# Mixing stage: queries and keys turned by DMA and joined by VectorE

## The reference, cut to what matters

```python
def hybrid_mixer(u, positions, w_in, b_gate, w_branch_moba, w_branch_sb, w_out):
    proj = u @ w_in                                   # 256 x 5120
    q_a, k_a, v_a, q_b, k_b, v_b, g_a, g_b = jnp.split(proj, cuts, axis=-1)
    q_a = partial_rotary(split_heads(q_a, N_HEADS_MOBA), positions)
    k_a = partial_rotary(split_heads(k_a, N_HEADS_MOBA), positions)
    y_a = merge_heads(moba_attention(q_a, k_a, split_heads(v_a, N_HEADS_MOBA)))
    y_b = merge_heads(stick_breaking_attention(split_heads(q_b, N_HEADS_SB),
                                               split_heads(k_b, N_HEADS_SB),
                                               split_heads(v_b, N_HEADS_SB)))
    gates = jax.nn.sigmoid(jnp.concatenate([g_a, g_b], axis=-1) + b_gate)
    merged = gate_a * (y_a @ w_branch_moba) + gate_b * (y_b @ w_branch_sb)
    return merged @ w_out
```

## Time and profile before

| | |
|---|---|
| median of 3 runs | 1204.53 us (1204.47 to 1204.54) |
| the profiled execution | 1204.95 us, its span 1203.0 us |
| TensorE busy | 1195.1 us, granted clock 1.00 in every slice |
| VectorE busy | 780.0 us |
| ScalarE busy | 699.0 us |
| mixing stage in the profile | about 186 to 345 us |

### The profile page before, as it was taken

The page is one execution under the profiler, slowest core; times in us unless marked ns, Lnnn a source line. Parts: engine busy times, 40 slices in busy tenths (PEclk is TensorE's granted clock), DMA queues, the critical chain, the costliest instruction groups (busy, mean ns, idle before and its releaser), DMA issues.

```text
span 1203.0 us, 16864 instructions
## 1 busy us (share of the span) xinstructions
PE 1195.1 (99%) x5622; PEld 986.0 (82%) x5622; DVE 780.0 (65%) x1107; ACT 699.0 (58%) x1030; POOL 73.8 (6%) x119
## 2 busy tenths in 40 slices
PE   9999999999999999999999999999999999999998
PEld 7888888877788888888888788888888887888887
DVE  6656556688686656557778766756556667665554
ACT  7545555566555545558675576645555546755552
POOL 0430000000000000000220110000000000000000
PEclk9999999999999999999999999999999999999999
DMA  9987764554556987755754528977655454876662
GB/s 314 268 235 228 224 200 153 162 168 139 164 193 190 275 248 231 220 179 174 200 171 162 175 60 230 262 226 210 205 175 175 144 163 132 245 225 200 202 200 76
DMA packets 218917, 234.68 MB, mean 195 GB/s; under 512 B 66608, under 2 KB 158896, under 8 KB 218864
## 3 DMA queue, kind: packets, MB, share of 16 engines
q1 hardware_dynamic: 163792, 214.61, 56.9%
q10 hardware_dynamic: 53280, 13.64, 6.3%
q0 software_dynamic: 1792, 5.75, 1.7%
HBM read 219.78 MB, written 1.05 MB: 184 GB/s over the span
## 4 chain that ended last, share of the span: by engine, by line
PE 96%; DMA 2%; DVE 1%; ACT 1%; issue 0%; ACTq 0%; DVEq 0%
PE bank L2035 30%; PE bank L2037 30%; PE bank L2036 30%; PE bank L2094 2%; DMA sb_probs<-sb_probs 1%; PE bank L2248 1%; PE bank L2264 1%; PE bank L2235 1%; PE bank L2233 0%; DMA sb_gates<-h_xT 0%; ACT sb_probs L1277 0%; PE bank L2552 0%; DVE sb_rmax L1930 0%; PE bank L2541 0%; PE bank L2266 0%
## 5 line engine op out<-in xcount | busy, mean ns | idle before, releaser
L1360 DVE TENSOR_TENSOR sb_wl<-sb_raw,sb_wh 128x1024 fp32r<-128x1024 f32 x313 | 376.3, 1222 | 116.5 <-ACT sb_wh L741 111.6
L2035 PE MATMUL bank<-sb_wh,sb_aTh 128*128 128x512 f32 (+1 forms) x1124 | 435.5, 387 | 0.6 <-DVE sb_scores L1423 0.5
L2037 PE MATMUL bank<-sb_wh,sb_aTl 128*128 128x512 f32 (+1 forms) x1124 | 431.0, 383 | 0.0
L2036 PE MATMUL bank<-sb_wl,sb_aTh 128*128 128x512 f32 (+1 forms) x1124 | 430.7, 383 | 0.0
L741 ACT ACTIVATE sb_wh<-sb_raw 128x1024 fp32r<-128x1024 f32 (+1 forms) x319 | 326.9, 1047 | 142.2 <-PE bank L2037 103.0
L2035 PEld LDWEIGHTS bank<-sb_wh,sb_aTh 128*128 128x128 f32 x1124 | 211.3, 188 | 42.2 <-issue 1.4
L2037 PEld LDWEIGHTS bank<-sb_wh,sb_aTl 128*128 128x128 f32 x1124 | 211.2, 188 | 41.9
L2036 PEld LDWEIGHTS bank<-sb_wl,sb_aTh 128*128 128x128 f32 x1124 | 211.4, 188 | 40.1
L1360 DVE TENSOR_TENSOR sb_wl<-sb_z,sb_wh 128x1024 fp32r<-128x1024 f32 x88 | 107.5, 1226 | 56.0 <-ACT sb_wh L741 56.0
L845 ACT ACTIVATE sb_junk<-bank,sb_rstd 128x256 f32<-128x256 f32 x88 | 36.8, 470 | 156.6 <-PE bank L2037 156.3
L1423 DVE SCALAR_TENSOR_TENSOR sb_scores<-bank,sb_rstd,sb_junk 128x256 f32<-128x256 f32 x88 | 38.5, 479 | 115.6 <-ACT sb_junk L845 115.4
(11 more groups left out here) (220 smaller groups left out, 929.1 us busy)
## 6 DMA issues: line engine op xcount, KB each, us to landing
sb_raw<-ffn_w_down SPq DMA_DIRECT2D x80, 256.0 KB, 4.4
sb_raw<-w_in SPq DMA_DIRECT2D x80, 256.0 KB, 3.2
sb_raw<-w_down SPq DMA_DIRECT2D x80, 256.0 KB, 3.9
sb_raw<-w_gate SPq DMA_DIRECT2D x48, 256.0 KB, 3.2
sb_raw<-w_up SPq DMA_DIRECT2D x48, 256.0 KB, 4.0
sb_raw<-ffn_w_gate SPq DMA_DIRECT2D x44, 256.0 KB, 3.6
sb_raw<-ffn_w_up SPq DMA_DIRECT2D x44, 256.0 KB, 4.4
sb_raw<-e_w_in SPq DMA_DIRECT2D x40, 256.0 KB, 3.3
```

Of the source, the lines that this page charges most:

```text
L1360: dve.tensor_tensor(wl[:, u % NSPLIT, :], raws[SLOT[u]], wh[:, u % NSPLIT, :].bitcast(F32), ALU.subtract).then_inc(low_done, 1)
L2035: pe.matmul(dst, lh, w_hi, start=start, stop=False)
L2036: pe.matmul(dst, lh, w_lo, start=False, stop=False)
L2037: return pe.matmul(dst, ll, w_hi, start=False, stop=stop)
```

## The change

TensorE no longer transposes the query and key tiles of the mixing stage. Instead, for each of the four tiles, ScalarE copies the 16-bit halves into a buffer (`qk_split`, two copies of 128x1024, at steps 4, 8, 17, 21) and issues one transposing DMA (`qk_turn`, at steps 5, 9, 19, 23), and VectorE joins the halves into `qkT` (`qk_join`, two copies of 128x1024, at steps 11, 12, 25, 27). TensorE waits for the first two joins ahead of unit 13 and for all four ahead of unit 29, where it had waited for evacuations ahead of units 13 and 25. The tiles used as buffers (`vm0`, `junk`, `qkT[:, 2]`, `qkT[:, 3]`) are free at these times; the fourth turn waits for the third, whose source it overwrites. The factor 0.125 moves from the copies into the addition of the mask: for mixing heads, one instruction multiplies the scores by 0.125 and adds the mask. The core of the diff (new semaphores and the removed code of `qt` and `qt_evac` are left out):

```diff
+        def as_halves(tile):
+            return tile.rearrange("p a c -> p (a c)").bitcast(U16)
+
+        QK_TILES = [0, 1, 3, 4]
+        qk_planes = [as_halves(a) for a in (vm0[:, :, :], qkT[:, 2, :, :], vm0[:, :, :])] + [junk[:, :].bitcast(U16)]
+        qk_planesT = [junk[:, :].bitcast(U16)] + [as_halves(a) for a in (qkT[:, 3, :, :], qkT[:, 3, :, :], vm0[:, :, :])]
...
+            def qk_split(k):
+
+                if k < 2:
+                    act.wait_ge(mix_evac_a, QK_TILES[k] + 1)
+                    act.wait_ge(mix_evac_d, QK_TILES[k] + 1)
+                else:
+                    act.wait_ge(rope_done, k - 1)
+                halves = z[:, :, QK_TILES[k], :].bitcast(U16).rearrange("p t (c h) -> p h t c", h=2)
+                for h in range(2):
+                    ins = copy(qk_planes[k].rearrange("p (h t c) -> p h t c", h=2, t=NT)[:, h], halves[:, h])
+                ins.then_inc(mix_planed, 1)
+
+            def qk_turn(k):
+
+                act.wait_ge(mix_planed, k + 1)
+                if k == 3:
+
+                    act.wait_ge(mix_turned[0], 32)
+                act.dma_start_transpose(qk_planesT[k].rearrange("p (b r) -> p b r", r=P), qk_planes[k]).then_inc(mix_turned[k % 2], 16)
 
...
             for v in range(4, 44):
-                if v == 6:
-                    qt_evac(mix_at, 0, 0.125)
-                if v == 10:
-                    qt_evac(mix_at, 1, 1.0)
+                split(u0 + v)
+                if v in (4, 8):
+                    qk_split(v // 4 - 1)
+                if v in (5, 9):
+                    qk_turn(v // 4 - 1)
+                if v in (17, 21):
+                    qk_split(v // 4 - 2)
+                if v == 19:
+                    qk_turn(2)
                 if v == 23:
-                    qt_evac(mix_at, 2, 0.125)
-                split(u0 + v)
-                if v == 23:
-                    qt_evac(mix_at, 3, 1.0)
+                    qk_turn(3)
                 mix_steps(v)
...
+            def qk_join(k):
+
+                dve.wait_ge(mix_turned[k % 2], 16 + 16 * (k // 2))
+                turned = qk_planesT[k].rearrange("p (h t k r) -> p h k t r", h=2, t=NT, k=4)
+                halves = as_halves(qkT[:, k, :, :]).rearrange("p (k t r h) -> p h k t r", k=4, t=NT, h=2)
+                for h in range(2):
+                    ins = dve.tensor_copy(halves[:, h], turned[:, h])
+                ins.then_inc(mix_joined, 1)
 
...
-                ins = dve.tensor_tensor(s, bank[4 + i % 2][:, 0:384], bias[:, :], ALU.add)
+                if kind == "fox":
+                    ins = dve.tensor_tensor(s, bank[4 + i % 2][:, 0:384], bias[:, :], ALU.add)
+                else:
+                    ins = dve.scalar_tensor_tensor(s, bank[4 + i % 2][:, 0:384], 0.125, bias[:, :], ALU.mult, ALU.add)
...
             for v in range(4, 44):
-                if v == 24:
-                    qt_evac(mix_at, 3, 1.0)
                 if v % 4 == 0 and v <= 24:
                     evac(u0 + v, W_IN_BANKS[v // 4 - 1], 1, z[:, :, v // 4 - 1, :], mix_evac_d)
                 if v in (16, 20):
                     rotate(v // 4 - 1)
-                if v == 6:
-                    qt_evac(mix_at, 0, 0.125)
-                if v == 10:
-                    qt_evac(mix_at, 1, 1.0)
-                if v == 23:
-                    qt_evac(mix_at, 2, 0.125)
                 if v < 13:
                     split(u0 + v)
                 elif v > 13:
                     split(u0 + v - 1)
+                if v in (11, 12):
+                    qk_join(v - 11)
                 mix_steps(v)
+                if v in (25, 27):
+                    qk_join((v - 21) // 2)
...
             for v in range(4, 44):
-                if v == 6:
-                    qt(mix_at, 0, 0, lambda: evacuated(1))
-                if v == 10:
-                    qt(mix_at, 1, 1, lambda: evacuated(2))
                 if v == 13:
 
                     evacuated(3)
-                    pe.wait_ge(mix_at.qt_evac_a, 2)
-                    pe.wait_ge(mix_at.qt_evac_d, 2)
-                if v == 23:
-
-                    pe.wait_ge(mix_at.s_read, 6)
-                    qt(mix_at, 2, 3, lambda: pe.wait_ge(rope_done, 1))
-                if v == 24:
-                    qt(mix_at, 3, 4, lambda: pe.wait_ge(rope_done, 2))
-                if v == 25:
-
-                    pe.wait_ge(mix_at.qt_evac_a, 4)
-                    pe.wait_ge(mix_at.qt_evac_d, 4)
+                    pe.wait_ge(mix_joined, 2)
+                if v == 29:
+
+                    pe.wait_ge(mix_joined, 4)
```

More of the change, by code:

```diff
@@ L341, in two_block_kernel @@
         dve_chain = sem("dve_chain")
+        mix_planed = sem("mix_planed")
+        mix_turned = [sem(f"mix_turned{i}") for i in range(2)]
+        mix_joined = sem("mix_joined")
         mix_evac_a = sem("mix_evac_a")
@@ L397, in __init__ @@
             def __init__(self, tag, stick=False, cross=False):
-                self.qt_psum = sem(tag + "_qt_psum")
-                self.qt_evac_a = sem(tag + "_qt_evac_a")
-                if not cross:
-                    self.qt_evac_d = sem(tag + "_qt_evac_d")
+                if not stick:
+                    self.qt_psum = sem(tag + "_qt_psum")
+                    self.qt_evac_a = sem(tag + "_qt_evac_a")
+                    if not cross:
+                        self.qt_evac_d = sem(tag + "_qt_evac_d")
                 self.s_psum = sem(tag + "_s_psum")
@@ L423, in two_block_kernel @@
         A_LAG = 3
-        QT_BANKS = [6, 6, 4, 4]
         MIX_SCORES = [13, 17, 21, 25, 29, 32, 35, 38]
@@ L987, in _ @@
             rstd_known(1)
-            def qt_evac(at, k, scale):
-                act.wait_ge(at.qt_psum, 2 * k + 1)
-                copy(qkT[:, k, 0:2, :], bank[QT_BANKS[k]][:, :], scale).then_inc(at.qt_evac_a, 1)
+            def qk_split(k):
[13 more added lines that the diff above has]
+                act.dma_start_transpose(qk_planesT[k].rearrange("p (b r) -> p b r", r=P), qk_planes[k]).then_inc(mix_turned[k % 2], 16)
             def mix_high(m):
@@ L1537, in evac @@
                 dve.tensor_scalar(dst[:, 1, :], bank[bank_ + 1][:, :], rs(stat, 1), None, ALU.mult).then_inc(done, 1)
-            def qt_evac(at, k, scale):
-                dve.wait_ge(at.qt_psum, 2 * k + 2)
-                dve.tensor_scalar(qkT[:, k, 2:4, :], bank[QT_BANKS[k] + 1][:, :].rearrange("p (h t) -> p h t", h=2), scale, None, ALU.mult)\
-                   .then_inc(at.qt_evac_d, 1)
+            def qk_join(k):
[5 more added lines that the diff above has]
+                ins.then_inc(mix_joined, 1)
             def rotate(m):
@@ L2200, in _ @@
             u0 = FIRST["w_in"]
-            def qt(at, k, m, ready):
-                ready()
-                if k >= 1:
-                    pe.wait_ge(at.qt_evac_a, k)
-                    pe.wait_ge(at.qt_evac_d, k)
-                for g in range(2):
-                    transposes(bank[QT_BANKS[k] + g], lambda j, t: z[:, t, m, tok(2 * g + j)]).then_inc(at.qt_psum, 1)
             def evacuated(n):
```

## The result

| | before | changed |
|---|---|---|
| median | 1204.53 us (1204.19 to 1205.08, 6 runs) | 1209.04 us (1206.17 to 1210.56, 6 runs) |
| profiled execution | 1204.95 us, span 1203.0 us | 1206.17 us, span 1204.4 us |

The ratio is 1.0034, 95% interval 1.0025 to 1.0044: slower by 4.5 us. The profiled execution, 1206.17 us, is the shortest of the six; the others go up to 1210.56 us, while the kernel before stays within 0.9 us. So the profile after shows the change at its best, and the spread needs an explanation of its own. I first read what the profile shows.

What follows compares the result with a forecast made beforehand. TensorE, busy 1195.1 of 1203.0 us, was taken to bound the kernel. The terms -3.5 + 3.2 + 1.3 = +1.0 us, added to 1204.53 us, gave 1205.5 us, range 1203.8 to 1208.0 us.

Steps and rivals of the forecast that it cites:

- Part 1: Mixing stage: removing TensorE's 32 transposes of four tiles saves 0.88 us a tile, -3.5 us before any new wait.
- Parts 2 and 3: Dropped evacuations of turned tiles on VectorE and ScalarE, and the factor moved into the mask's addition: 0 us each.
- Part 5: Step 13: TensorE waits ahead of unit 13 for tile 1's join, queued behind unit 16's low half on VectorE: +3.2 us.
- Part 6: Step 29: TensorE waits ahead of unit 29 for VectorE's joins 2 and 3: +1.3 us.
- Part 4: ScalarE's splits and turning DMAs fit into its idle time, landing within 8.2 us: 0 us.
- Rival (a): The hole at step 13 lowers TensorE's clock to 1.2 GHz: +1.9 us or a little more, 1207.4 us; chance 0.17.
- (d): Transfers come late: a turn lands over 11 us after start or delays a weight unit: +2 us, 1207.5 us; chance 0.09.

Runs made afterwards that it cites:

- moba_by_dma: Changed kernel, but only tiles 2 and 3 turned by DMA, 0 and 1 by TensorE as before, joins' wait behind unit 29's products: 1203.63 us, ratio 0.9994.
- no_turns_behind: waits_behind without the first two turning DMAs; joins of tiles 0 and 1 read unturned halves, so the output differs: 1202.64 us, ratio 0.9985.
- all_behind: waits_behind with TensorE's wait for tile 2's evacuation also behind unit 13's products and ScalarE's table load behind unit 16's high half: 1201.92 us, ratio 0.9988.
- before_hole: Kernel before the change, plus two join-shaped VectorE copies at step 12 that TensorE awaits ahead of unit 13; no added turns: 1209.62 us, ratio 1.0043.
- fill13: Changed kernel with 14 needless TensorE products directly ahead of its wait for joins 0 and 1, before unit 13: 1207.0 us, ratio 1.0022.
- join1_first: Changed kernel with tile 1's join moved ahead of unit 16's low half in VectorE's queue at step 12: 1209.62 us, ratio 1.0036.
- waits_behind: Changed kernel with TensorE's two waits for joins moved behind the products of units 13 and 29: 1202.92 us (1201.73 to 1207.99), ratio 0.9997.
- sb_by_dma: Changed kernel, but only tiles 0 and 1 turned by DMA, 2 and 3 by TensorE as before, joins' wait behind unit 13's products: 1205.53 us, ratio 1.0015.
- two_more_turns: moba_by_dma plus two needless 0.5 MB turning DMAs issued by ScalarE at steps 31 and 34: 1202.46 us, ratio 0.9986.
- turn0_later: all_behind with tile 0's turning DMA issued at ScalarE's step 7 instead of 5: 1205.51 us (1201.20 to 1207.54), ratio 1.0005.
- after_again: The changed kernel measured once more, nothing altered: 1208.55 us (1207.12 to 1212.19), ratio 1.0035; the profiled execution took 1210.55 us.

## Why the prediction was wrong, point by point

**Part 1 (-3.5 us): right.** moba_by_dma gains 1.80 us in the stage for two tiles, where two times 0.88 was said. The mark that I gave for it, TensorE busy 3.5 us less, was poor: it is 2.3 us less, 3.0 us in the stage, since the last product ahead of a hole and the first behind it count longer than their distance of 0.23 us, and 0.7 us more in the rest of the kernel, which the change doesn't touch. The stage of no_turns_behind, with all four tiles off TensorE, is 3.3 us shorter.

**Parts 2 and 3 (0 us): nothing speaks against them.** The stage of all_behind, -2.9 us with a hole of 0.7 us, leaves no room for another price. They weren't tested by themselves.

**Part 5 (+3.2 us): right in place and size** for the execution profiled first, 3.5 us, and for the hole made in the kernel before, 3.3 us. In before_hole it is also right in its chain: VectorE idles 2.3 us for ScalarE's high half ahead of the low half. In the changed kernel another chain ended last, VectorE's own work since 220.65 us with join 0 in it, which the sum had left out; that it came out only 0.14 us behind the one foretold is luck. And 3.5 us is the smallest of the holes in the profiles of the changed kernel and its near kin, not the only one.

**Part 6 (+1.3 us): right,** 1.1 us, ended by join 3.

So the sum of the parts, +1.0 us, is what the profile shows, +1.3 us in the stage and 1206.17 us in all; and the median is 1209.04 us. The prediction was a sum over an execution in which nothing goes late.

**Part 4 (0 us) is the step that failed,** and with it the clock, which the sum put at nothing and left to a rival (next paragraph). I gave the turning DMAs "room" because ScalarE had idled 3.43 us, and took 8.2 us as the longest landing. The rows with 1.33 and 3.6 us of held queue were there, and I took them for a spread without a cause. In fact the first turn holds the queue for 3.8 to 5.4 us in every profile that has it at step 5, it lands after 8.8 to 13.1 us in the profiles of the changed kernel, the repeat, fill13 and join1_first, and beside it a weight load that took 4.8 us takes 11.0 to 11.6 us in the long executions. ScalarE waited for these loads before, in three waits up to 209 us; I concluded that TensorE would not feel more, because those units are used from 211 us on. In the long executions ScalarE's wait moves to 211 to 215 us and reaches the hole of part 5, which grows from 3.3 to 5.3 and 6.5 us. With the first two turns four of the twelve executions of waits_behind and two of the eleven of sb_by_dma are long (over 1206 us, at a lowered clock); of the kernels that issue no turn at steps 5 and 9 (no_turns_behind, moba_by_dma, two_more_turns) none of thirty-three is. The mark that I had set for this, ScalarE waiting for DMAs after 209 us, is met there and not in the first profile.

**Rival (a) was priced right and given too small a chance.** I said 1.9 us for a fallen clock; eight products at half pace cost 1.7 us. (The products at the kernel's start, from which the price was read, run at half pace while the granted clock of that stretch is given as 1.00; the pace is what the price rests on.) Against it stood that the clock is 1.00 past the short holes; but holes of up to 1.3 us say nothing on one of 3.2 us. In before_hole the mean clock fell in four of five executions.

**Rivals (a) and (d) are not alternatives.** A late transfer makes the hole longer, and the longer hole lowers the clock more surely: in the 1210.55 us execution 3.2 us more hole and 1.7 us of clock, together 4.9 us, where the stage is 4.8 us longer than in the first profile. I gave each a time with the other left out, and so no case came to the 1209 us measured. How the 4.5 us of the median divide can't be read from one profile. From before_hole, 5.1 us for a hole that costs 3.3 us, the clock's share is about 1.8 us; with the +1.3 us of the sum that leaves about 1.4 us for late transfers. This division is worked out, not measured. By it the clock alone would have given 1207.6 us, still inside the range that I stated; the late transfers of part 4 take the median out of it.

**What stays open.** Why the same program has its first turn land after 8.8 us in one execution and 12.5 us in another; the DMA engines are full there (share 0.98 to 1.09), and small shifts may decide who is first, but no run shows it. Whether the held queue or the traffic does more of the harm: turns issued from another engine's queue would part them, and no run has that. And what the long executions of waits_behind, all_behind and turn0_later look like.

## What to carry to other kernels

Put a wait in front of the first instruction that reads the data, not in front of the work ahead of it: moving two waits, each behind one unit's products, was worth some 6 us here, more than the 3.5 us that the change was about. A transposing DMA isn't only its two copies and a landing time: count what it holds in the issuing engine's queue and what loads it meets, and look for several rows of it before taking one. And when each of two hazards would lengthen the same hole, price them together.

## What the runs showed of the hardware

A hole of 3.3 us in TensorE's work lowered the mean granted clock in four of five executions, and at half pace the first eight products cost 1.7 us; in the profiles, holes of up to 2.2 us from start to start (turn0_later) left it at 1.00, those of 3.5 and 3.7 us (before_hole and the changed kernel, the shortest execution of each) did too, and those of 4.5 us (fill13) and 6.9 us (after_again) lowered it to 0.50 and 0.51.

A transposing DMA of 0.5 MB from ScalarE's queue holds it either for 1.3 to 1.4 us or for 1.8 to 4.6 us (5.4 at most), and the count of transposing DMAs before it goes with which. Over all 14 profiles the fast ones of this size are the 15th, 23rd and 27th of an execution, whatever stage they fall in; the 12th to 14th, 24th to 26th, 28th and 30th are slow. Every fourth would fit this, but only the step from two to four more was tested by a run made for it. Those of 0.25 MB take 1.25 us at nearly every place, 2.3 us at most. By the Trainium skill (Advanced Engine Details and Errata, "X-Bar Transpose (TRN2)") transposing DMAs are as fast as regular ones; here, in the changed kernel's profile, a weight unit of the same 0.5 MB, issued in two halves at 204.4 and 204.8 us, had landed 5.2 us after the first issue, and the turns beside such loads took 8.8 and 7.8 us (7.1 to 13.1 us over all profiles). So this case doesn't agree where the two meet.
